# One 1024-column subtraction per weight block instead of two of 512 columns

## What is computed

```
for l in range(2):
    h = rms_norm(x)
    proj = h @ w_in[l]                      # 50 blocks of 128 output columns
    o_lru, o_diff, o_swa = three mixers(proj)
    gates = sigmoid(h @ w_gate[l] + b)      # 24 blocks
    up = branches @ w_branch[l]             # 24 blocks
    x = x + sum(gates * up) @ w_out[l]      # 8 blocks
    h2 = rms_norm(x)
    q = h2 @ w_q[l]                         # 16 blocks
    pick 16 experts in each of 8 heads from q; weights g
    x = x + (g * gelu(h2 @ u.T)) @ v        # 128 blocks of u, 128 blocks of v
return rms_norm(x)
```

## Time and profile before

| what | value |
| --- | --- |
| median of 3 runs | 2462.65 us (2459.61 to 2463.94) |
| span of the profiled execution | 2461.2 us |
| PE busy | 2372.8 us, 96% of the span, 16310 matmuls |
| DVE busy | 1667.5 us, 68%, 3882 instructions |
| ACT busy | 1447.1 us, 59%, 3296 instructions |
| POOL busy | 498.6 us, 20% |
| DMA | 449.67 MB, mean 183 GB/s |
| TensorE clock granted, mean | 0.992 |

### The profile page before, as it was taken

One profiled execution on the slowest core, in us unless ns is written; L12 is line 12 of the kernel. 1 busy time (PEld: TensorE's weight loads), 2 busy tenths in 40 slices (PEclk: granted clock), 3 DMA queues, 4 the chain that ended last, 5 costly groups with the idle time before them and its releaser, 6 DMA issues.

```text
span 2461.2 us, 50127 instructions
## 1 busy us (share of the span) xinstructions
PE 2372.8 (96%) x16310; PEld 2175.1 (88%) x16314; DVE 1667.5 (68%) x3882; ACT 1447.1 (59%) x3296; POOL 498.6 (20%) x417
## 2 busy tenths in 40 slices
PE   8998989999999999999999989899999999999998
PEld 8997888999999878888899978889999998788887
DVE  5667775577876676666656667755778767666666
ACT  5576755555655655555555676555555556555555
POOL 0000200007767400000000003000177773000000
PEclk9999999999999999999999999999999999999999
DMA  5554465456666446566544535654566664466664
GB/s 207 191 186 142 167 246 177 152 180 187 172 188 172 137 145 222 216 210 220 198 148 171 175 134 203 213 179 154 179 184 176 187 182 109 171 221 213 219 216 162
DMA packets 165203, 449.67 MB, mean 183 GB/s; under 512 B 48060, under 2 KB 58228, under 8 KB 164852
## 3 DMA queue, kind: packets, MB, share of 16 engines
q1 hardware_dynamic: 115860, 412.44, 48.3%
q0 software_dynamic: 46080, 33.71, 6.9%
q10 hardware_dynamic: 3168, 2.39, 0.4%
HBM read 429.44 MB, written 21.66 MB: 183 GB/s over the span
## 4 chain that ended last, share of the span: by engine, by line
PE 87%; ACT 5%; DVE 5%; issue 2%; DMA 2%; ACTq 0%; POOL 0%; DVEq 0%; POOLq 0%; SPq 0%
PE bank L301 16%; PE bank L303 16%; PE bank L302 16%; PE bank L316 10%; PE bank L318 10%; PE bank L317 10%; PE bank L1613 2%; DVE w_lo L283 2%; ACT w_hi L270 2%; DMA raw<-stream 1%; ACT L343 1%; PE bank L393 1%; PE bank L1073 1%; PE bank L1595 1%; PE bank L1046 1%
## 5 line engine op out<-in xcount | busy, mean ns | idle before, releaser
L283 DVE TENSOR_TENSOR w_lo<-raw,w_hi 128x512 fp32r<-128x512 f32 x1512 | 1027.6, 690 | 718.2 <-ACT w_hi L270 704.6
L270 ACT ACTIVATE w_hi<-raw 128x512 fp32r<-128x512 f32 x1512 | 904.5, 626 | 384.7 <-PE bank L318 313.0
L301 PE MATMUL bank<-h_hi,w_hi 128*128 128x256 f32 x3360 | 963.6, 287 | 14.1 <-DVE w_lo L283 13.9
L302 PE MATMUL bank<-h_lo,w_hi 128*128 128x256 f32 x3360 | 952.5, 283 | 0.0
L303 PE MATMUL bank<-h_hi,w_lo 128*128 128x256 f32 x3360 | 952.4, 283 | 0.0
L301 PEld LDWEIGHTS bank<-h_hi,w_hi 128*128 128x128 f32 x3360 | 646.2, 192 | 25.9 <-DVE w_lo L283 18.8
L302 PEld LDWEIGHTS bank<-h_lo,w_hi 128*128 128x128 f32 x3360 | 646.8, 193 | 0.5
L303 PEld LDWEIGHTS bank<-h_hi,w_lo 128*128 128x128 f32 x3360 | 646.5, 192 | 0.0
L1204 POOL DMA_INDIRECT spread_w<-mass,cell_at x256 | 429.1, 1676 | 444.7 <-DVE mass L1491 298.0
L316 PE MATMUL bank<-w_hi,a_hi 128*128 128x512 f32 x1088 | 426.9, 392 | 10.6 <-DVE a_lo L411 5.6
L317 PE MATMUL bank<-w_lo,a_hi 128*128 128x512 f32 x1088 | 426.0, 392 | 0.0
(11 more groups left out here) (196 smaller groups left out, 1956.4 us busy)
## 6 DMA issues: line engine op xcount, KB each, us to landing
raw<-stream SPq DMA_DIRECT2D x378, 1024.0 KB
spread_w<-zeros POOLq DMA_DIRECT2D x32, 512.0 KB, 15.2
h_hi<-spread_w POOLq DMA_DIRECT2D x32, 512.0 KB, 4.8
hank<-rel_hankel SPq DMA_DIRECT2D x16, 256.0 KB, 2.6
spread_w<-mass,cell_at POOLq DMA_INDIRECT x256
rel_hankel<-rel_line SPq DMA_DIRECT2D x16, 192.0 KB
hank<-rel_hankel SPq DMA_DIRECT2D x16, 128.0 KB, 2.1
A<-subkeys SPq DMA_DIRECT2D x2, 1024.0 KB, 5.9
```

What stands on the lines that cost most here:

```text
L270: act.activation(w_hi[:, (ring % 2) * 2 + k, :], raw[:, slot, sub, 512 * k:512 * k + 512], ACT.Copy).then_inc(w_hi_done, 1)
L283: dve.tensor_tensor(w_lo[:, q, :], raw[:, slot, sub, 512 * k:512 * k + 512], w_hi[:, q, :].bitcast(F32), ALU.subtract).then_inc(w_parts, 1)
L301: pe.matmul(ps, hi, rhs_hi(4 * k + c), start=first, stop=False)
L302: pe.matmul(ps, hi, rhs_lo(4 * k + c), start=False, stop=False)
```

## The change

`split_lo` no longer calls `split_half` twice. It waits for both high halves of the block and subtracts all 1024 columns in one instruction, which raises `w_parts` by 2 at its end. `split_half` itself stays, and so do its direct callers. ACT still makes the high part in halves.

```diff
         def split_lo(dve, b, r):
 
-            for k in range(2):
-                split_half(dve, b, r, k)
+            blk, ring = b + place.first, (r + place.first) % 4
+            slot, sub = ring // 2, ring % 2
+            q = (ring % 2) * 2
+            dve.wait_ge(w_hi_done, blk * 2 + 2)
+            whole_block = w_hi[:, q:q + 2, :].rearrange("p a b -> p (a b)")
+            dve.tensor_tensor(w_lo[:, q:q + 2, :].rearrange("p a b -> p (a b)"), raw[:, slot, sub, :], whole_block.bitcast(F32), ALU.subtract).then_inc(w_parts, 2)
```

## The result

The changed kernel takes **2497.7 us** (2495.1 to 2500.4, 4 runs) against 2461.1 us of the kernel before in the same rounds (2457.7 to 2463.9). The ratio is 1.0148 (95% interval 1.0134 to 1.0163): 36.6 us slower. The profiled execution has a span of 2494.5 us, 33.3 more than before.

A forecast was written before the change was run, and what follows sets the result against it. PE holds 87% of the chain and DVE waits for ACT, so what counts is how late a block's first half is ready. Two layers at 8.9 us give 17.8, plus 4 in `v`: 22 us, 2484.5 us (own range 2478 to 2491; overall 2474 to 2498).

The forecast's parts named there:

- rival 4: `v` stretch becomes DVE-bound: instruction 1.3 us or PE's register wait 0.15 more; 15 us in place of 4, 2499 us; 15%.
- DVE's saving is off the path: All blocks: DVE busy falls by 67 us, within time its wait already covers, so worth nothing by itself.
- DVE starting 0.03 us behind a copy: All whole blocks: subtraction starts 0.03 us after ACT's second copy; half 0 is ready 1.05 us later than before.
- up blocks: Blocks 2 to 8, 42 to 49 and last `u` blocks: 0.14 us lost once in two blocks, 1.1 us per layer.
- The turns: `w_out` with the turn to block 106, and the turn to layer 1: predicted loss 0.
- Branch products: Blocks 83 to 97: 1.3 us at block 86, 0.5 at 89, 0.7 over 92 to 97; 2.4 us per layer.
- Query projection: 14 blocks per layer: seven losses, mostly 0.26 us, two 0.51 at loop returns, one 0.14; 2.2 us per layer.
- Places just in time: Block 33 and two last `u` places: half 0 about 1 us late; with 0.3 more, 3.2 us per layer.
- Block 50 swallowed: Block 50 is late by 1 us, but PE idles longer before block 51 for ACT's table load; no loss.
- The wait of PE in `v`: `v` stretch: PE's register wait before the load adds 0.05 to 0.09 us; the stretch loses 4 us in both layers.
- Loads: SP's load release comes 0.53 us later; no cost, up to 10 us if the cover before second copies is gone.
- Row and rule: Two skill rules disagree on joining DVE instructions; the rows decide: 67 us gained off the path, 22 lost on it.

The follow-up runs named there:

- experiments 3: Against the kernel before: whole-block subtraction in the `v` stretch alone, raising a semaphore of its own by 1, halves elsewhere; 2465.88 us, ratio 1.0024.
- experiment 5: Kernel before, still two 512-column subtractions, but the first half waits for both high halves; 2474.32 us against 2458.38, ratio 1.0057.
- experiment 4: Against the kernel before: whole blocks in the query projection alone, 14 a layer, own semaphore raised by 1, halves elsewhere; 2466.24 us in a single run.
- experiment 10: Changed kernel with halves again for 17 blocks a layer: 33, 37, 41, 45, the last `u` blocks from 235 and block 250; 2490.67 us against 2459.23.
- the turned order: Kernel before, halves kept; next half-layer's first low part moved behind the norm's diagonals, sums into `x` earlier; 2455.70 us against 2458.38, again 2460.13 against 2459.23.

## Why the prediction was right, and what it mis-sized

Direction, mechanism and most places held. It predicted 22 us, and 36.6 came. The time lies inside the range to 2498 by 0.3 us, which is luck: two of the four runs lie above it, and the median is above the forecast's own range to 2491. It is close to the 2499 of rival 4, but not for its reasons: the instruction takes 1.226 us, not 1.3, and the `v` stretch as a whole cost 8 us, not 15.

- **DVE's saving is off the path: right.** 53 us of DVE work went, and no stretch got faster by it. I had said 67: the 832 halves that went were busy 562 us (1027.6 - 465.2) and not 574, since back-to-back halves overlap, and the new instruction took 1226 ns. For the same reason the 0.16 us a block in my branch term is 0.07 where two halves run back to back (1.29 against 1.22).
- **"DVE starting 0.03 us behind a copy": this step failed.** It is 0.10 for the instruction that raises its semaphore by 2 (experiments 3 and 4), and for those halves of the kernel before that do not carry their wait; I had read one half that does. It enters every path from ACT's second copy to a late load. In `v` it took the loss from 4.3 us to 8.1. In the up blocks 0.14 became 0.22 to 0.24, in the query projection 0.26 became 0.36. As an estimate, with some 25 such paths a layer, 50 x 0.07 = 3.5 us, and 3.8 in `v`: 7 of the 15 us that were missing.
- **The turns were left out: this step failed too.** I listed blocks whose weight load is late for PE, and never asked what stands behind a low part on DVE's own queue. At three places it is the sums into `x`: 3 x 0.6, and 2 x 1.4 of clock, 4.6 us in all. With the 7 of the gap and 0.8 in layer 0's query projection that is 12.4, less the 1.3 by which the branch products of this one trace stay under their term; the 11.3 us by which the span exceeded the 22 are then accounted for. That the clock belongs to the late norm is a count over traces, 8 of 10 against 0 of 14, and not shown one by one.
- **Branch products: a just-in-time place was taken for a loss that vanishes.** I had let losses ahead of block 86 disappear in its wait for a load. But PE already waited for half 0 of block 83 in the kernel before (0.97 us, shown below the table of places). Block 83 starts 1.13 and 1.17 us later in the changed kernel, and 1.1 to 1.4 later in all ten such stretches; with the wait alone (experiment 5) it is 0.52 and 0.46. How much of it the load's wait takes back varies from trace to trace, which is why the term of 2.4 us a layer met 1.6 to 5.1, 3.3 on average. Twice that average less twice this trace's 1.75 is 3.0 us, the size of what the medians show beyond the spans.
- **Query projection: size off.** 3.42 and 2.63 for 2.2; layer 1's surplus is the gap. Layer 0's further 0.8 is for the most part DVE starting 0.46 us behind the copy once and 0.23 twice (experiment 4); why it does stays open.
- **Places just in time: right.** Block 33 1.13 (1.04 predicted), block 248 1.12 (1.0), block 241 0.76 and 1.01 (0.9). Experiment 10 puts halves back there, and the loss there goes.
- **Block 50 swallowed: right.** Blocks 42 to 50 lost 1.77, block 51 gave 1.12 back.
- **The wait of PE in `v`: right.** From the activation's low part to the load 0.14 us, within the 0.05 + 0.05 to 0.09 that I took. The trace has a register instruction of PE's between them (1016.41 to 1016.45 behind an end at 1016.37, load at 1016.50).
- **Loads: right so far as tested.** ACT's waits for `raw` rose from 29.5 to 79.4 us, the largest change in the table of waits, and cost nothing that I can find. They fall on first copies: one that ended at 1016.36 was followed by a second that PE held until 1016.83. The kernel with the whole instruction everywhere but in `v` and `w_out` has 24.9 us of such waits and still loses 29.5. No run moved the loads alone.
- **Row and rule.** The Trainium skill, "Perfetto Trace Analysis", Optimizing Scalar/DVE Operations, says that breaking up instructions of an unsaturated engine may complete work sooner; the joined instruction agrees (+36.6 us), and experiment 5, where the instructions stay broken up but wait together (+15.9), says that the early first half is a good part of it. The Trainium skill, "VectorE: DVE Perf Modes", on the TRN2 errata, has a fixed latency that one large tile pays once and small ones each; that is real here too (1226 ns against 2 x 688), and worth nothing.

## What to carry to other kernels

Two halves of an intermediate that another engine consumes in order are a pipeline; before joining them, find for each consumer how much room the first half has, and count what else stands behind the producer on its own queue. An engine that idles 700 us has time to spare for work, but the path through it may have none: that its work is cheap does not make its latency cheap. Look at whether a wait still rides on its instruction: here a sequencer instruction of its own cost each such path 0.07 us. And before a stretch is judged by one trace of each kernel, see how much it moves between kernels that are alike there.

## What I had not expected of the hardware

- A DVE subtraction that raises its semaphore by 2 does not carry its wait: a semaphore instruction of its own stands ahead, and the work starts 0.10 us behind the copy that releases it. With a raise by 1, on a semaphore of its own, it starts 0.03 behind (222 of 222 waits against 238 of 238). The same 0.10 stands at 46 halves of the kernel before that raise by 1 but have a second condition to wait for, so it belongs to the separate instruction.
- With a norm that ended 0.6 us later came a 3.4 us stretch at half the granted clock (1.2 GHz), 19 matmuls in place of 29 and 1.4 us lost: 8 of 10 times at blocks 106 and 484, 0 of 14 times with the norm in time. So 0.6 us on the path became 2.0, twice. Such falls come at other places too (9 in the kernel before, 11 in the changed one, without the one at each kernel's very end) and not the same in each execution: the turned order has 7 in one trace and 10 in the other.
